# First projection group of a two-layer decoder trunk: queries and keys in one interleaved walk, on one Trainium2 core

## What is computed

```python
def moba_mixer(hn, w_in, w_out):
    proj = hn @ w_in                       # 256 x 2048 @ 2048 x 8192
    q, k, v, z = jnp.split(proj, 4, axis=-1)
    q, k, v = apply_rope(to_heads(q)), apply_rope(to_heads(k)), to_heads(v)
    o = moba_attention(q, k, v)            # softmax(q k^T) v, causal
    return (o * jax.nn.silu(z)) @ w_out

def reference(x, ...):
    for i in range(DEPTH):                 # DEPTH = 2
        hn = rms_norm(x, pre_norm_g[i])
        y = mixer_i(hn)
        x = x + rms_norm(y, post_norm_g[i])
```

## Time and profile before

| | us |
|---|---|
| median of 3 runs (847.71 to 851.01) | 850.21 |
| the profiled execution | 850.66 |
| its span, first to last instruction | 848.9 |
| PE busy | 837.6 |
| DVE busy | 684.5 |
| ACT busy | 428.2 |
| POOL busy | 336.4 |

### The profile page before, as it was taken

One profiled execution on the slowest core, in us unless ns is written; L12 is line 12 of the kernel. 1 busy time (PEld: TensorE's weight loads), 2 busy tenths in 40 slices (PEclk: granted clock), 3 DMA queues, 4 the chain that ended last, 5 costly groups with the idle time before them and its releaser, 6 DMA issues.

```text
span 848.9 us, 12103 instructions
## 1 busy us (share of the span) xinstructions
PE 837.6 (99%) x3873; PEld 695.4 (82%) x3873; DVE 684.5 (81%) x1179; ACT 428.2 (50%) x592; POOL 336.4 (40%) x169
## 2 busy tenths in 40 slices
PE   8999999999999999999999999999999999999996
PEld 6888888888888888888888788888888888888884
DVE  4688799988999799968656629999999999566555
ACT  5744544455444645454445674545444554574441
POOL 0243004500441014400000299888888878772000
PEclk9999999999999999999999999999999999999999
DMA  9956655656467545746655366555655546556522
GB/s 320 293 164 199 195 151 171 194 182 198 150 189 213 188 150 170 225 148 219 215 188 193 129 199 199 187 174 184 198 179 172 194 156 198 191 212 236 197 98 99
DMA packets 97509, 159.49 MB, mean 188 GB/s; under 512 B 3300, under 2 KB 38468, under 8 KB 97092
## 3 DMA queue, kind: packets, MB, share of 16 engines
q1 hardware_dynamic: 97284, 158.97, 58.5%
q10 hardware_dynamic: 192, 0.08, 0.0%
HBM read 156.94 MB, written 2.10 MB: 187 GB/s over the span
## 4 chain that ended last, share of the span: by engine, by line
PE 97%; issue 1%; DMA 1%; DVE 0%; ACT 0%; DVEq 0%; POOLq 0%; POOL 0%; ACTq 0%
PE acc L420 29%; PE acc L422 29%; PE acc L421 29%; PE X L430 2%; PE acc L405 1%; PE acc L407 1%; PE acc L406 1%; PE acc L501 1%; PE acc L486 1%; DMA ident<-in_identity 1%; PE X L560 0%; PE X L545 0%; PE X L544 0%; PE X L561 0%; PE X L559 0%
## 5 line engine op out<-in xcount | busy, mean ns | idle before, releaser
L773 ACT ACTIVATE w_hi<-raw 128x1024 fp32r<-128x1024 f32 x282 | 298.8, 1061 | 354.4 <-PE acc L422 354.0
L420 PE MATMUL acc<-w_hi,xT_hi 128*128 128x512 f32 x864 | 339.0, 392 | 0.1
L422 PE MATMUL acc<-w_hi,xT_lo 128*128 128x512 f32 x864 | 336.5, 389 | 0.0
L421 PE MATMUL acc<-w_lo,xT_hi 128*128 128x512 f32 x864 | 336.2, 389 | 0.0
L1059 DVE TENSOR_TENSOR w_lo<-raw,w_hi 128x1024 fp32r<-128x1024 f32 x182 | 245.7, 1366 | 78.9 <-ACT w_hi L773 76.6
L1518 POOL TENSOR_TENSOR w_lo<-raw,w_hi 128x1024 fp32r<-128x1024 f32 x100 | 243.1, 2438 | 48.9 <-ACT w_hi L773 48.7
L422 PEld LDWEIGHTS acc<-w_hi,xT_lo 128*128 128x128 f32 x864 | 162.2, 188 | 34.0
L420 PEld LDWEIGHTS acc<-w_hi,xT_hi 128*128 128x128 f32 x864 | 162.3, 188 | 33.1 <-DVE xT_lo L1078 0.3
L421 PEld LDWEIGHTS acc<-w_lo,xT_hi 128*128 128x128 f32 x864 | 162.3, 188 | 32.9
L1343 DVE SCALAR_TENSOR_TENSOR X<-u_pad,taps,X 128x256 f32<-128x256 f32 x464 | 182.5, 480 | 0.0
L1481 POOL TENSOR_TENSOR small<-small 128x1 f32<-128x1 f32 (+1 forms) x7 | 4.3, 618 | 232.9 <-DVE small L1289 124.2
(11 more groups left out here) (151 smaller groups left out, 755.0 us busy)
## 6 DMA issues: line engine op xcount, KB each, us to landing
raw<-in_w_in SPq DMA_DIRECT2D x78, 1024.0 KB, 5.3
raw<-in_w_in SPq DMA_DIRECT2D x66, 512.0 KB, 4.4
raw<-in_w_out SPq DMA_DIRECT2D x32, 1024.0 KB, 5.0
gpost<-in_post_g SPq DMA_DIRECT2D x2, 1024.0 KB, 5.0
xrow<-in_x SPq DMA_DIRECT2D x4, 256.0 KB, 5.5
raw<-in_w_in SPq DMA_DIRECT2D x4, 256.0 KB, 4.9
xrow<-in_x SPq DMA_DIRECT2D x2, 512.0 KB, 10.0
bout<-in_b_out SPq DMA_DIRECT2D x1, 1024.0 KB, 7.3
```

Of the source, the lines that this page charges most:

```text
L420: nc.tensor.matmul(a, hi[:, k, rows], w_hi[:, slot, i], start=(k == 0), stop=False)
L421: nc.tensor.matmul(a, hi[:, k, rows], w_lo[:, slot, i], start=False, stop=False)
L422: last = nc.tensor.matmul(a, lo[:, k, rows], w_hi[:, slot, i], start=False, stop=(k == KT - 1))
L773: nc.scalar.activation(w_hi[:, slot], raw[:, u % LOADS, 2 * half:2 * half + 2], ACT.Copy).then_inc(hi_ready[slot], 1)
```

## The change

Slices 0 to 15 of the first group are walked in the order `TWO_BLOCKS`: two slices of q, the same two k-slices of k, the next two of q, and so on, into both halves of `acc`. Each pair of x tiles then serves two slices, and x is transposed in three runs of eight after slices 2, 5 and 9. Slices 2 and 3 no longer run in passes. ACT and DVE prepare 14 slices (`PREPARED`) before the loop, with the split of x behind slices 5, 9 and 13. q is complete after slice 13; ACT copies it out at s = 17, and DVE turns it at s = 20 to 23 (`TURN_Q_FIRST`), k as before at 24 to 27. The transposes of the small vectors move from s = 9 to s = 17. The identity is loaded first on SP instead of second on ACT's queue, and the nine matmuls on zeros are cut into 4, 3 and 2 around the first transposes.

```diff
-SPLIT_AFTER = ((), (), (2,), (3,), (4, 5), (6,), (7, 8), (9,))
-SQUARES_AFTER = (1, 2, 3, 5)
-STAGED = 4
+TWO_BLOCKS = tuple((n, k + i) for k in (0, 2, 4, 6) for n in (0, 1) for i in (0, 1))
+PREPARED = 14
+SQUARES_AFTER = {7: (0, 1), 8: (2,), 10: (3, 4), 11: (5,), 12: (6,), 13: (7,)}
+TURN_Q_FIRST = 20
...
+            sp.dma_start(ident[:], identity).then_inc(ident_in, 16)
             x_load(0, 0)
...
             w_load(0, 3, 3, raw_ready[0])
+            w_load(1, 0, 1, half_in, D)
+            w_load(1, 2, 3, raw_ready[1], D)
             x_load(2, 2)
-            w_load(1, 0, 1, half_in)
             x_load(3, 3)
-            w_load(1, 2, 3, raw_ready[1])
+            two_block_load(2)
             x_load(4, 5)
-            load(S_QKVZ, 0, 32, 2, w_in0[0], 0)
+            two_block_load(3)
             x_load(6, 7)
-            load(S_QKVZ, 0, 32, 3, w_in0[0], 0)
-            load(S_QKVZ, 0, 32, 4, w_in0[0], D)
+            two_block_load(4)
...
+                for s in range(2, 2 * SLICES):
+                    n, part = TWO_BLOCKS[s]
+                    if n == 0:
+                        pe.wait_ge(xlo_ready, part + 1)
+                    slice_products(S_QKVZ, 0, 32, s, xT_hi, xT_lo, (n, part))
+                    if s in (2, 5, 9):
+                        h = 2 + 2 * (2, 5, 9).index(s)
+                        input_T(0, h)
+                        input_T(0, h + 1)
...
-            keep_clock(7)
+            keep_clock(4)
             pe.wait_ge(ident_in, 16)
             pe.wait_ge(pre_in, 16)
             nc.tensor.transpose(X[3][:, 0:NPRE], ...).then_inc(vec_T, 1)
+            keep_clock(3)
             input_T(0, 0)
-            first_block()
+            keep_clock(2)
+            first_blocks()
...
-                    if s == 9 and first:
+                    if s == 17 and first:
...
-            act.dma_start(ident[:], identity).then_inc(ident_in, 16)
...
+            for s in range(FINE, PREPARED):
+                high(S_QKVZ, 0, 32, s)
+                if s in (5, 9, 13):
+                    h = 2 + 2 * (5, 9, 13).index(s)
                     input_high(0, h, V_PRE0)
+                    input_high(0, h + 1, V_PRE0)
...
-                    if s == 11:
-                        if first:
-                            act.wait_ge(rms_ready, 1)
+                    if s == 17 and first:
+                        act.wait_ge(rms_ready, 1)
+                        block_rows(S_QKVZ, g, 32, 7, q_row, rms[0], at=13)
+                    if s == 11 and not first:
                         block_rows(S_QKVZ, g, 32, 7, q_row, rms[0])
...
+                turn_q = TURN_Q_FIRST if first else TURN_Q
```

More of the change, by code:

```diff
@@ L309, in x_load, with w_load, two_block_load @@
                 sp.dma_start(xrow[:, :, c], xv[:, :, c]).then_inc(x_in[x_chunk(first)], 16)
-            def w_load(n, first, last, done):
-                k = 2 * SL_K * n
-                sp.dma_start(raw[:, n, first:last + 1], wv[:, k + first:k + last + 1, 0:NCOL]).then_inc(done, 16)
+            def w_load(n, first, last, done, col=0):
+                sp.dma_start(raw[:, n, first:last + 1], wv[:, first:last + 1, col:col + NCOL]).then_inc(done, 16)
+            def two_block_load(j):
+                n, part = TWO_BLOCKS[2 * j]
+                load(S_QKVZ, 0, 32, j, w_in0[0], n * D, part // 2)
+            sp.dma_start(ident[:], identity).then_inc(ident_in, 16)
             x_load(0, 0)
@@ L339, in _ @@
                          .rearrange("(q r) c -> r q c", r=DW_ROWS)).then_inc(dw_in, 16)
-            for j in range(5, 16):
+            for j in range(5, 8):
+                two_block_load(j)
+            for j in range(8, 16):
                 load(S_QKVZ, 0, 32, j, w_in0[0], (j // 4) * D)
@@ L471, in input_T @@
                     pair_T(xrow, X[h % 4], 2 * h).then_inc(xT_done, 1)
[L473 to L488, removed]
             def tile_products(t):
@@ L504, in tile_products, with first_blocks @@
                     last.then_inc(w_used[slot], 1)
-            def first_block():
+            def first_blocks():
                 tile_products(0)
                 input_T(0, 1)
[L510 to L522, removed]
+                for t in (1, 2, 3):
+                    tile_products(t)
+                for s in range(2, 2 * SLICES):
[7 more added lines that the diff above has]
+                        input_T(0, h + 1)
             def keep_clock(n):
@@ L565, in group @@
             def group(g, first):
-                for s in range(SLICES if first else 0, 4 * SLICES):
-                    if s % SLICES == 0 and not (first and s < 2 * SLICES):
+                for s in range(2 * SLICES if first else 0, 4 * SLICES):
+                    if s % SLICES == 0:
                         pe.wait_ge(rows_out, 4 * g + s // SLICES - 1)
@@ L774, in high, with block_rows @@
                                      ).then_inc(hi_ready[slot], 1)
-            def block_rows(first, it, per, s, dst, scale, func=ACT.Copy):
-                act.wait_ge(w_used[RING - 1], rounds(first, it, per, s))
+            def block_rows(first, it, per, s, dst, scale, func=ACT.Copy, at=None):
+                at = s if at is None else at
+                act.wait_ge(w_used[at % RING], rounds(first, it, per, at))
                 par = ((first + s) // SLICES) % 2
@@ L841, in tile_high @@
                                      ).then_inc(hi_ready[h] if c else tile_whi, 1)
[L843 to L847, removed]
+            for t in range(2 * FINE):
+                tile_high(t)
+            for s in range(FINE, PREPARED):
+                high(S_QKVZ, 0, 32, s)
+                if s in (5, 9, 13):
+                    h = 2 + 2 * (5, 9, 13).index(s)
                     input_high(0, h, V_PRE0)
[L849 to L852, removed]
+                    input_high(0, h + 1, V_PRE0)
+                for n in SQUARES_AFTER.get(s, ()):
                     wait_columns(n // 2)
                     input_squares(junk0[:], n // 2, n % 2, n)
-            for n in range(len(SQUARES_AFTER), SLICES):
-                wait_columns(n // 2)
-                input_squares(junk0[:], n // 2, n % 2, n)
             def heads_high(g):
@@ L884, in group @@
             def group(g, first):
-                for s in range(SLICES + LEAD if first else 0, 4 * SLICES):
+                for s in range(PREPARED if first else 0, 4 * SLICES):
                     high(S_QKVZ, g, 32, s)
@@ L888, in group @@
                         group_end(s, g - 1)
-                    if s == 12 and first:
+                    if s == 20 and first:
                         act.wait_ge(vec_T, 2)
@@ L1112, in tile_low @@
                                         ).then_inc(lo_ready[h] if c else tile_wlo, 1)
[L1114 to L1118, removed]
+            for t in range(2 * FINE):
+                tile_low(t)
+            for s in range(FINE, PREPARED):
+                low(S_QKVZ, 0, 32, s)
+                if s in (5, 9, 13):
+                    h = 2 + 2 * (5, 9, 13).index(s)
                     input_low(0, h, V_PRE0)
-                for s in SPLIT_AFTER[h]:
-                    low(S_QKVZ, 0, 32, s)
+                    input_low(0, h + 1, V_PRE0)
             dve.wait_ge(rope_in, 48)
@@ L1221, in group @@
                         group_end(s, g - 1)
-                    if s in range(TURN_Q, TURN_Q + 4):
-                        if s == TURN_Q:
+                    if s in range(turn_q, turn_q + 4):
+                        if s == turn_q:
                             dve.wait_ge(rope_step, 6 * g + 3)
@@ L1226, in group @@
                                 dve.wait_ge(s_done, G * g)
-                        turn(qT, q_row, s - TURN_Q, qT_ready)
+                        turn(qT, q_row, s - turn_q, qT_ready)
                     if s in range(TURN_K, TURN_K + 4):
```

## The result

| | before | changed |
|---|---|---|
| median of 13 runs each (us) | 849.14 (847.52 to 851.01) | 851.35 (850.58 to 852.86) |
| the profiled execution | 850.66 | 852.85 |
| its span | 848.9 | 851.1 |
| share of PE in the chain that ended last (profiled execution) | 97% | 90% |

The ratio is 1.0032, 95% interval 1.0024 to 1.0040: the change costs 0.24 to 0.40%, inside the 0.5% that were called "no change", and by its interval a loss. The forecast for the median was 851.2 us.

A forecast was written before the change was run, and what follows sets the result against it. PE bounds the kernel, 97% of the 848.9 us span. Start -2.4, wait before the scores +3.3, handover 0.1: +1.0 us on the profiled 850.66, 851.7; median 0.45 below, 851.2 us. Range 848.0 to 854.0.

The forecast's parts named there:

- The start of PE: At kernel start: first product at 6.9 instead of 7.40, 0.5 us sooner, with PE's clock rising at 10.0 instead of 12.1.
- slice 4 cannot start before 20.2: First group, slice 4: loading and preparing unit 2's weights sets its earliest start at 20.2; 20.6 was forecast.
- A gain of 2.4 us if nothing waits.: From the start through slice 16: 55.0 plus 0.44 for moved small-vector transposes, 55.4 against 57.82, 2.4 us gained.
- The turns of q: Before the first scores: q's rotation ends at 63.0, eight turns follow, `kT` is ready at 88.6; PE waits 3.3 us.
- The rule of shared bandwidth: Lows beside POOL's rotation: alternative to the exclusive lock, 0.5 proportionally for each of three lows, excess 1.6, sum +0.3 us.
- Rival A: Before the scores: lows slip between POOL's steps, excess near 0, PE waits 1 us, sum -1.4, 848.8 us; chance 0.20.
- Rival B: At the scores: PE's clock falls in the new wait, costing 3.1 us, sum +4.1, 854.3 us; chance 0.08.
- Rival C: At the start: clock rises at 12.1 as before, slice 4 starts at 21.7, everything behind 1.1 later, 852.3 us; chance 0.15.
- The longer runs themselves bring nothing: x transposes in the first group: a run of eight costs 0.87 us, twice the 0.44 of a run of four.
- Cost nothing behind the scores: Behind the first scores: DVE reaches the maxima about 1.5 us later, but PE's next wait is over 15 us on.

## Why the prediction was right, and where it was off

*The time, the range and the sign held*: 851.2 forecast, 851.35 measured. The mechanism held too, a wait for the turned keys that eats the gain at the start. The size of the change did not: +1.0 us was forecast, +2.2 measured. That the time came out so close is in part luck. It was 850.66 - 2.4 + 3.4 - 0.45, with 3.4 for the wait and its handover. The 3.4 was 0.6 us too large, and the 0.45 taken off for the median did not hold for the changed kernel, whose profile with the clock up is at 851.15 and whose median is at 851.35; these two errors cancelled.

*The start of PE, "0.5 us sooner" and "I take 10.0" for the clock.* In the profile the first product came at 5.99, not 6.9, and the clock was up before 7. The identity alone landed 2.0 us after its issue, where I had taken about 3.0, from the 3.2 of a transfer four times its size. All this was cut off by the floor that I did give: "slice 4 cannot start before 20.2", with 20.6 as the value; it started at 20.42, and the run with half units shows that this floor is unit 2's.

*"A gain of 2.4 us if nothing waits."* Right against the profile shown, with 55.01 + 0.44 against 57.82. Wrong as a term for the median: the second profile of before has its scores 2.55 us sooner, and the median lies between. 849.1 is 1.5 us under the profiled 850.66, so the typical gain is 2.4 - 1.5 = 0.9 us. This is the term that was mis-sized. In the forecast time it did no harm, since the late start stands in the 850.66 as well as in the 2.4. I had set the median 0.45 under the profiled run, from three runs; with thirteen it is 1.5. The three runs shown, 847.71 to 851.01, held the warning: their spread of 3.3 us was larger than the whole term.

*The turns of q, "the term that decides".* Its steps came out one by one: POOL from 52.12 (52.1), end at 62.9 (63.0), lows lengthened by 0.3, 0 and 1.65 (0.4, 0.2 and 1.7), `kT` at 88.05 (88.6). The wait in all was 2.8 us instead of 3.3. The runs without k's rotation and with only the late turns confirm both of its parts. The lock that the Trainium skill states in "SBUF — State Buffer", section "Who interferes with whom", fits here: a low of 2.88 us beside POOL's last step and of 1.22 without it, POOL's step of 2.30 us beside the low at 68.11, which itself was not longer, while the turns stayed at 1.77 to 1.80. The rule of shared bandwidth would have given 1.7 each for three lows, and 1.53, 1.23 and 2.88 were measured.

*The sum at the median* then reads -0.9 + 2.8 = +1.9 us. The three executions of 13 in which the clock falls raise the median by only 0.1, since the other ten have theirs at 851.27. That makes 2.0, where 2.2 were measured between the medians. The forecast's +1.0 lay on a base of 850.2 that was itself 1.1 too high.

*Rival A* (no excess) is out. *Rival B* (the clock falls in the new wait) came true in some executions, at 1.7 us and not 3.1, so its price was too high and its condition no matter of yes or no; the long pause at the start, from which the price was taken, was no measure of it. The Trainium skill tells in "TensorE: Matmul & The Clock Gate", section "HAM oscillation", of waits that put the clock back; the rows at 0.50 above agree, and the second profile, with the same wait and no fall, shows that a wait of 2.0 us need not. *Rival C* (the start brings nothing) was stated for the wrong reason, a clock that rises late, but the run with the old start shows its substance: in the changed kernel the new start brings nothing that can be measured.

*"The longer runs themselves bring nothing"*: a run of eight took 0.87 us in the chain; as forecast. *"Cost nothing behind the scores"*: no wait of PE behind them in the list of waits.

## What to carry to other kernels

Where an in-order queue takes more per step than the bound engine (3.06 us against 2.72 here), space its heavy steps out: moved together, eight of them outlast their slack. Moving work later is not free if its input has its own long chain; follow copy-out, rotation and turn to the next consumer before choosing the place. And before a gain is read off one profile, look where that execution lies among its runs: here the profiled one started late, and most of the gain at its start was there in the median already.

## What the runs showed of the hardware

- With a wait of 2.0 us between matmuls the granted clock fell to 0.50 in one execution of the changed kernel and stayed at 1.00 in another; of all five profiles with a wait of 1.9 to 2.0 us, two show the fall. It cost 1.7 us in both. After 0.65 and 0.68 us it did not fall in the two profiles that had such a wait.
- The clock at a kernel's start varies between executions of one binary: up at about 12.1 in one run of before, by 5.2 in another, and this and the first transfers made all of the 2.5 us between them. The granted clock is printed as 1.00 in both. In the profile with only the late turns, whose start is that of before, four transposes at 5.69 took 0.66 us, the upper level, and from 8 to 10 the clock is printed as 0.50: it had risen and fallen again.
- A GpSimd step and a VectorE subtract of two SBUF tensors exclude each other in both directions: the low waited 1.65 us for POOL's last step, a POOL step beside a low took 2.30 us where its twin took 1.25, and POOL's first four steps took 4.80 us instead of 3.80 once one more low fell among them. VectorE's 32x32 transposes beside the same steps were not longer.
